# Two RMS norms of a two-block kernel: square sums from a product with a block of ones, spread over the partitions at once

## What is computed

```python
# first block
x = x + mx[:, :, 2] * yx                                   # yx ends in a product with w_out
h2 = modulate(rmsnorm(x, norm2_g), mx[:, :, 3], mx[:, :, 4])   # h * (1 + scale) + shift
x = x + mx[:, :, 5] * conv_ffn(h2, ffn_up, ...)            # 1024 -> 5632, 3x3 convolution, gate, -> 1024
# second block
x = x + mix @ w_out_2
h2 = rms_norm(x, norm2_g_2)
f = square(relu(h2 @ w_mlp1_2))                            # 1024 -> 4096
x = x + f @ w_mlp2_2
```

## Time and profile before

| what | value |
|---|---|
| median of 3 runs | 802.79 us (801.47 to 807.8) |
| the profiled execution, its own time | 803.1 us |
| its span in the profile | 801.3 us |
| mean granted TensorE clock in it | 0.967 of full speed |
| PE busy | 751.8 us, 94% of the span |
| DVE, POOL, ACT busy | 580.5, 368.8, 352.2 us |
| bytes moved by DMA | 144.61 MB, mean 180 GB/s |

### The profile page before, as it was taken

One profiled execution on the slowest core, in us unless ns is written; L12 is line 12 of the kernel. 1 busy time (PEld: TensorE's weight loads), 2 busy tenths in 40 slices (PEclk: granted clock), 3 DMA queues, 4 the chain that ended last, 5 costly groups with the idle time before them and its releaser, 6 DMA issues.

```text
span 801.3 us, 13939 instructions
## 1 busy us (share of the span) xinstructions
PE 751.8 (94%) x5892; PEld 717.7 (90%) x5892; DVE 580.5 (72%) x911; ACT 352.2 (44%) x424; POOL 368.8 (46%) x90
## 2 busy tenths in 40 slices
PE   8779979988999898999999998999799999999998
PEld 3467869988899898999999997999689999999998
DVE  5989995999602645999999998253966765556553
ACT  5443413345254255655545555433455433443331
POOL 0154542344546675888887886564627400000000
PEclk9889998999999998999999999999989999999999
DMA  9943945565324443764555544334215365445611
GB/s 375 421 159 138 343 161 219 171 220 205 133 106 158 158 159 114 287 211 166 203 180 194 207 162 160 148 113 155 105 54 203 121 255 198 171 167 202 211 53 53
DMA packets 20658, 144.61 MB, mean 180 GB/s; under 512 B 2290, under 2 KB 2546, under 8 KB 3444
## 3 DMA queue, kind: packets, MB, share of 16 engines
q1 hardware_dynamic: 20448, 143.64, 49.5%
q10 hardware_dynamic: 148, 0.07, 0.0%
HBM read 142.66 MB, written 1.05 MB: 179 GB/s over the span
## 4 chain that ended last, share of the span: by engine, by line
PE 56%; DVE 36%; issue 4%; ACT 2%; DMA 2%; SPq 0%; DVEq 0%; ACTq 0%
PE bank L1313 15%; PE bank L1315 15%; PE bank L1314 15%; DVE Y L1076 14%; DVE AL L1089 5%; PE bank L1331 3%; DVE raw L839 2%; PE bank L1421 2%; DVE F L950 1%; DMA XR<-in_xT 1%; DVE PM L1191 1%; DVE QF L913 1%; DVE XS L891 1%; DVE ada_s L785 1%; DVE wlo L359 1%
## 5 line engine op out<-in xcount | busy, mean ns | idle before, releaser
L359 POOL TENSOR_TENSOR wlo<-raw,whi 128x2048 fp32r<-128x2048 f32 (+1 forms) x79 | 362.8, 4599 | 269.6 <-ACT whi L445 266.2
L445 ACT ACTIVATE whi<-raw 128x2048 fp32r<-128x2048 f32 x107 | 204.1, 1910 | 80.2 <-PE bank L1315 46.0
L1076 DVE SCALAR_TENSOR_TENSOR Y<-bank,vec,Y 128x189 f32<-128x189 f32 (+2 forms) x352 | 121.1, 417 | 4.0 <-ACT Y L637 3.9
L1313 PE MATMUL bank<-H2h,whi 128*128 128x256 f32 x352 | 99.5, 283 | 1.7 <-DVE H2l L1052 1.7
L1314 PE MATMUL bank<-H2l,whi 128*128 128x256 f32 x352 | 99.2, 282 | 0.0
L1315 PE MATMUL bank<-H2h,wlo 128*128 128x256 f32 x352 | 99.2, 282 | 0.0
L359 DVE TENSOR_TENSOR wlo<-raw,whi 128x2048 fp32r<-128x2048 f32 (+1 forms) x33 | 72.4, 2196 | 35.0 <-ACT whi L445 35.0
L1313 PE MATMUL bank<-H1h,whi 128*128 128x256 f32 (+1 forms) x288 | 91.4, 317 | 6.6 <-issue 5.9
L1314 PE MATMUL bank<-H1l,whi 128*128 128x256 f32 (+1 forms) x288 | 89.4, 310 | 0.0
L1315 PE MATMUL bank<-H1h,wlo 128*128 128x256 f32 (+1 forms) x288 | 89.1, 309 | 0.0
L1313 PE MATMUL bank<-H4h,whi 128*128 128x256 f32 x256 | 72.0, 281 | 0.7 <-issue 0.7
(11 more groups left out here) (264 smaller groups left out, 1908.1 us busy)
## 6 DMA issues: line engine op xcount, KB each, us to landing
raw<-in_w_mlp SPq DMA_DIRECT2D x32, 1024.0 KB, 4.8
raw<-in_w_in SPq DMA_DIRECT2D x30, 1024.0 KB, 4.9
raw<-in_ffn_up SPq DMA_DIRECT2D x22, 1024.0 KB, 4.9
raw<-in_ada_hi SPq DMA_DIRECT2D x16, 1024.0 KB, 5.1
raw<-in_ffn_down SPq DMA_DIRECT2D x11, 1024.0 KB, 4.8
raw<-in_w_out SPq DMA_DIRECT2D x8, 1024.0 KB, 4.9
ada_s<-in_ada_s SPq DMA_DIRECT2D x4, 1024.0 KB, 13.8
ada_p<-in_ada_p SPq DMA_DIRECT2D x3, 1024.0 KB, 13.9
```

The lines of the kernel that those rows point to most:

```text
L359: e.tensor_tensor(wlo[q % NHI][:, cols], raw[place[split[q]] % NRAW][:, cols], whi[q % NHI][:, cols].bitcast(F32), ALU.subtract).then_inc( ...
L445: e.activation(whi[q % NHI][:, :], raw[n % NRAW][:, :], ACT.Copy).then_inc(s["w_hi"], 1)
L1076: e.scalar_tensor_tensor(o[:, r0:r1, c0:c1], z[:, r0 + dr:r1 + dr, c0 + dc:c1 + dc], cw[:, f, tap:tap + 1], o[:, r0:r1, c0:c1], ALU.mult, ...
L1313: e.matmul(out, h[:, col:col + P], xh, start=first, stop=False, skip_group_check=True)
```

## The change

Both norms lose the column sums and the spreading product. `square_rows` has the ones as the stationary operand (128x128) and a whole square tile of 256 tokens as the moving one: the sum over the features comes out on all 128 partitions, in one bank, from 4 products accumulated. ACT then takes the root of 128x256 in place in that bank (`root_rows`), and DVE the reciprocal of 128x256: for norm 1 in place in the bank, for norm 3 from the bank into `RR`, which replaces ACT's copy. `row1` and `rows3` are gone from the bank tables. The entry `norm1` holds its bank until `h2_mul` is 8 (all eight `TMP1` products done), `norm3` until `rstd_x` is 2. The two entries `norm1` and `norm3` stand in the places of `col1` and `col3`, so they get the same banks, 7 and 6.

```diff
-MISC += [(f"rdo_row{n}", "rdo_gain", 2 * n + 2) for n in range(2)] + [("col1", "rms_x", 1)]
+MISC += [(f"rdo_row{n}", "rdo_gain", 2 * n + 2) for n in range(2)] + [("norm1", "h2_mul", 8)]
...
-MISC2 += [(f"av{n}", "mix_lo", n + 3) for n in range(2)] + [("col3", "rms_x", 2), ("rows3", "rr_done", 3)]
+MISC2 += [(f"av{n}", "mix_lo", n + 3) for n in range(2)] + [("norm3", "rstd_x", 2)]
...
-    where["row1"], before["row1"] = 3, last[3]
     acc1 = [last[b] for b in (4, 5, 6, 7)]
-    where["col2"], before["col2"] = 3, ("h2_mul", 8)
+    where["col2"], before["col2"] = 3, last[3]
...
+        def root_rows(name):
+            b = bank[misc_bank[name]][:, 0:T]
+            e.activation(b, b, ACT.Sqrt, bias=eps[:, 0:1], scale=1.0 / D).then_inc(s["rms_x"], 1)
...
-        e.wait_ge(s["col_x"], 1)
-        root(misc_bank["col1"], 2, D, 0, "rms_x")
+        e.wait_ge(s["row_x"], 1)
+        root_rows("norm1")
         warm(ACT.Silu)
...
         high(turn["w_mlp1", 0] + 2)
-        e.wait_ge(s["col_x"], 2)
-        root(misc_bank["col3"], 2, D, 0, "rms_x")
         e.wait_ge(s["row_x"], 3)
-        e.activation(RR[:, :], bank[misc_bank["rows3"]][:, 0:T], ACT.Copy).then_inc(s["rr_done"], 1)
+        root_rows("norm3")
...
-        reciprocal(2, 0, ("rms_x", 1), "rstd_x")
-        e.wait_ge(s["row_x"], 1)
+        norm1 = bank[misc_bank["norm1"]][:, 0:T]
+        e.wait_ge(s["rms_x"], 1)
+        e.reciprocal(norm1, norm1).then_inc(s["rstd_x"], 1)
+        e.wait_ge(s["rstd_x"], 1)
...
-            e.scalar_tensor_tensor(TMP1[:, k, :], XR[:, k, :], A2[:, k:k + 1], bank[misc_bank["row1"]][:, 0:T],
+            e.scalar_tensor_tensor(TMP1[:, k, :], XR[:, k, :], A2[:, k:k + 1], norm1,
                                    ALU.mult, ALU.mult).then_inc(s["h2_mul"], 1)
...
-        reciprocal(2, 0, ("rms_x", 2), "rstd_x")
+        e.wait_ge(s["rms_x"], 2)
+        e.reciprocal(RR[:, :], bank[misc_bank["norm3"]][:, 0:T]).then_inc(s["rstd_x"], 1)
...
-                    e.wait_ge(s["rr_done"], 3)
+                    e.wait_ge(s["rstd_x"], 2)
...
-        def square_columns(b, sq, f, n):
+        def square_rows(b, sq, f, n):
             for k in range(f, f + n):
-                for t in range(2):
-                    m = e.matmul(b[:, t:t + 1], sq[:, k, t * P:(t + 1) * P], ones[:, 0:1], start=k + t == 0,
-                                 stop=k == KT - 1, skip_group_check=True)
+                m = e.matmul(b[:, 0:T], ones[:, 0:P], sq[:, k, :], start=k == 0, stop=k == KT - 1)
             return m
...
         for j in range(2):
             e.wait_ge(s["sq1"], 4 + j)
-            m = square_columns(bs, SQ1, 6 + j, 1)
-        m.then_inc(s["col_x"], 1)
-        b = misc("row1")
-        e.wait_ge(s["rstd_x"], 1)
-        rows(b, [wide(0), wide(1)], "row_x")
+            m = square_rows(bs, SQ1, 6 + j, 1)
+        m.then_inc(s["row_x"], 1)
...
         for i in range(18):
             if i < 16:
                 pair("w_mlp1", i, H4h, H4l, ready=h4_ready if i == 0 else None,
                      midway=finish_norm if i == 0 else None)
-                if i == 0:
-                    b = misc("rows3")
-                    e.wait_ge(s["rstd_x"], 2)
-                    rows(b, [wide(0), wide(1)], "row_x")
```

More of the change, by code:

```diff
@@ L165 @@
 qk_rms qk_rstd k_row k_norm val_2 score_mm score row_max exp exp_rstd prob pt_mm pt_done x_norm pool_step pool_mm
-pool_out conv_2 mix_hi mix_lo av x3 sq3 h4_hi h4_lo sq3_sum relu square f_hi f_lo tables_in late_in col_x rms_x
+pool_out conv_2 mix_hi mix_lo av x3 sq3 h4_hi h4_lo sq3_sum relu square f_hi f_lo tables_in late_in rms_x
 rstd_x row_x""".split()
@@ L1573, in merged @@
             e.wait_ge(s["mg_lo"], k // 2 + 1)
-        bs = misc("col1")
+        bs = misc("norm1")
         for i in range(3):
@@ L1579, in tensor @@
         e.wait_ge(s["sq1_sum"], 2)
-        square_columns(bs, SQ1, 0, 2)
+        square_rows(bs, SQ1, 0, 2)
         for j in range(2):
             e.wait_ge(s["sq1"], 4 + j)
-            m = square_columns(bs, SQ1, 6 + j, 1)
-        m.then_inc(s["col_x"], 1)
-        b = misc("row1")
-        e.wait_ge(s["rstd_x"], 1)
-        rows(b, [wide(0), wide(1)], "row_x")
+            m = square_rows(bs, SQ1, 6 + j, 1)
+        m.then_inc(s["row_x"], 1)
         def h2_ready(k):
@@ L1730, in tensor @@
         order2 = [6, 7, 4, 5, 0, 1, 2, 3]
-        bs = misc("col3")
+        bs = misc("norm3")
         for i in range(3):
@@ L1735, in tensor @@
         e.wait_ge(s["sq3_sum"], 2)
-        square_columns(bs, SQ3, 0, 2)
+        square_rows(bs, SQ3, 0, 2)
         def h4_ready(k):
@@ L1744, in finish_norm @@
                 e.wait_ge(s["sq3"], 4 + j)
-                m = square_columns(bs, SQ3, 6 + j, 1)
-            m.then_inc(s["col_x"], 1)
+                m = square_rows(bs, SQ3, 6 + j, 1)
+            m.then_inc(s["row_x"], 1)
         for i in range(18):
```

## The result

The changed kernel takes 809.01 us (median of 13 runs, 805.4 to 812.17), the kernel before, on the same chips, 801.62 us (13 runs, 799.97 to 807.8). The ratio is 1.0073, with a 95% interval of 1.0051 to 1.0095: slower by 4.1 to 7.6 us, 5.9 in the middle. The two medians themselves lie 7.4 us apart, the two means 6.1. Forecast were +4.4 us and 807.5 us. The profiled execution took 811.15 us, with a span of 809.4 us against 801.3.

The account below looks back on a forecast made before the run. PE, never out of work in the feed-forward stage from 307.2, was taken as the bound. +4.4 us by pair 0's end and 0 at norm 3, on the profiled 803.1 us, gave 807.5 us, range 803.3 to 810.2.

Parts of the forecast that it names:

- The wait is the cost: PE's first `ffn_up` matmul waits for the eighth `TMP1`, ending at 311.42 before other delays, instead of `H2l` at 307.10.
- Rival B: At `ffn_up`, PE still starts with the first `H2l`; only root, reciprocal and spreading count: +0.8 us, 803.9 us; chance 6%.
- The first `TMP1`: At norm 1, longer root and reciprocal less the spreading start it at 306.38 against 305.55, +0.83 us.
- PE's start: PE's first `ffn_up` matmul starts at 312.38 instead of 307.23, +5.15 us.
- The clock: After its start on `ffn_up`, PE runs 3.4 us at half clock, losing 1.7 us; before, 4.9 us, losing 2.45.
- Pair 0: The first `ffn_up` pair ends at 319.68 instead of 315.28, +4.4 us; ends +3.8 to +5.4 us.
- All after it moves along: All work after pair 0 moves by the same time, so +4.4 us is carried to the end.
- rival A: At PE's 3.72 us wait before 499.39, up to 3.7 us come back: 803.8 us; chance 11%.
- The time itself: Profiled execution of 803.1 us plus 4.4 us gives 807.5 us.
- Norm 3 gives nothing: PE's 0.4 us saved is waited away before `w_mlp1` pair 3, wait 1.1 us; gain 0, at best 0.4 us.
- Rival C: At norm 3 the reciprocal into `RR` stands behind POOL; PE's wait grows by 2.6 us: 810.1 us; chance 8%.
- The table load as the next cover: At norm 1, with a cheap reciprocal, ACT's table load holds `H2h` until about 306.3 against 306.06: still +0.25 us.

Follow-up runs that it names:

- experiments 1 and 5: Changed kernel with norm 1's sums in bank 3: ratio 1.0004; changed kernel with PE's `acc1` wait moved to its first `ffn_down` product: ratio 1.0000.
- experiment 2: Kernel before with only the wait for `h2_mul` 8 added to `acc1`: 807.79 us, ratio 1.0057.
- experiment 8: Kernel before and changed kernel each profiled once more, no edit: 801.19 and 808.72 us.
- the profile of 842 us: Profile of a slow execution, 842.12 us: changed kernel with norm 1 in bank 3, one-operation inverse root on ACT, Silu's table load behind the first `Y`.
- experiment 3: Kernel before with only norm 3 changed, nothing at norm 1: 801.92 us, ratio 0.9989.
- experiment 4: Changed kernel with norm 1's reciprocal on 2 numbers a partition instead of 256, the norm's division left out: 808.1 us, ratio 1.0066.
- experiment 6: Changed kernel, norm 1 in bank 3, one-operation inverse root on ACT, Silu's table load later: six of 14 executions 841.79 to 842.99 us, others 799.13 to 804.54.

## Why the prediction was right, and where it was off

*The wait is the cost.* Right. Taking it away brings the time back to before's (experiments 1 and 5, 24 runs), adding it alone to the kernel before gives +4.6 us (2.4 to 6.7) of the change's +5.9 us (experiment 2). Rival B, that it isn't a wait, is out.

*The first `TMP1`.* Forecast +0.83 us, measured +0.91 us (+0.79 between the profiles of experiment 8). The root took 0.45 us (0.51 assumed), the reciprocal 1.77 us (1.61 from the slope of the small ones, 0.42 and 1.9 as ends). The slope through 2 numbers at 166 ns and 256 at 1,766 ns is 6.3 ns a number. What the Trainium skill suggests in VectorE: DVE Perf Modes, "First, the fixed hardware budget", a repeat count of 8, made 2.3 us as an estimate if each repeat were a cycle; the trace doesn't bear that out, since 1.77 us were measured. At the page's 0.96 GHz, 6.3 ns would be about six cycles, an estimate. What the trace does agree with is that the reciprocal takes longer than an ordinary operation of 256 elements (0.42 us).

*PE's start.* Forecast +5.15 us, measured +5.50 us (8.59 against 3.09; +5.28 us, 8.50 against 3.22, in the second pair of profiles). The missing part is mostly the hand-over: 0.13 us were assumed behind the last `TMP1`, it was 0.3 to 0.4 us. Other waits of PE's queue stand behind the one that held it; that they take the time was not tried.

*The clock.* From PE's start to ACT's first `Y` 5.6 us are work at full clock. The loss over that was 2.05 and 1.6 us after the change, forecast 1.7; before 2.5 and 2.4 us. In the other kernels it lay between 1.6 and 3.1 us, but for the profile of 842 us: there the clock was 1.00 and 0.8 us were still lost, since PE had to wait 0.79 us from one `H2l` to the next. The choice of 3.4 us at half clock was near, by luck in part: the same kernel shows losses 0.45 us apart.

*Pair 0.* Forecast +4.4 us, measured +5.05 and +4.5 us. The term that was too small is the start of PE, by 0.35 and 0.13 us.

*All after it moves along.* Held through the `ffn_up` stage and up to the second block's projections: PE's wait there is 3.7 us in all these profiles, so rival A didn't come. Behind that wait it didn't hold exactly. The longer half clock cost another 0.6 and 1.3 us in the two pairs of profiles (experiment 8), a term that the sum doesn't have. The times of all runs say +5.9 us with 4.1 at the low end; the forecast of +4.4 lies within that, on its lower side. This half clock is the best candidate for the missing 1.5 us, but as it came without the late start too, and not with each, its mean share is open.

*The time itself.* That 807.5 us lies only 1.5 us under the measured median is luck in part: the sum started from a profiled execution of 803.1 us, and the kernel before has a median of 801.62 us.

*Norm 3 gives nothing.* Right, to the size of the wait: 1.1 us forecast, 1.18 us measured after the change and 1.19 in experiment 3. Rival C, a reciprocal behind POOL, is out: it took 1.76 us while POOL worked.

*The table load as the next cover.* Right (experiment 4).

## What to carry to other kernels

A longer hold of a buffer costs where its release is waited for, not where the buffer is used next. When a table of banks or a pool gets a later release, look for every place that waits for "all of them", above all ahead of the engine that bounds the stage, and put the wait at the first use. Fewer instructions on an engine that afterwards waits for another can be worth nothing, as at norm 3; follow that wait back first. And a reciprocal of a value already spread over the partitions costs by its length: here 256 numbers took 1.77 us, 2 took 0.17.

## What the runs showed that was not expected

A version that starts the stage 0.9 us earlier lost 40 us in some executions (experiment 6). In the one such profile two engines, DVE and POOL, get in each other's way in nearly every turn instead of every second; that the start of the stage chooses between the two is a theory that fits the profiles. None of the timed executions of the kernel before or of the one with only the late table load showed it.

PE's gapless matmul rhythm takes one of two values in a stage, 0.1166 or 0.1176 us at full granted clock, 1.5 us over the `ffn_up` stage and as much over the last one, and the same kernel shows both. What chooses was not found.

The half clock after one and the same wait of 3.7 us lasted for 3.3 or for 5 to 6 us of PE's work. What chooses was not found either.
